# RWKV chunk recurrence: separate 64-row products become stacked 128-row products

## The chip, the cores and the metric

The kernel runs on one core of a Trainium2 chip, in one launch. The metric is the device time in microseconds; lower is better. All data is fp32 in memory.
## The reference

The model has two layers on 256 tokens of width 2048. Layer 0 has eight heads of stick-breaking attention and sixteen heads (of 64 channels) of an RWKV-7 recurrence; layer 1 is a gated delta net; each is followed by a squared-ReLU MLP of width 8192. Only the RWKV part matters here:

```python
def step(S, inp):
    r_t, w_t, k_t, v_t, kk_t, a_t = inp
    s_kk = jnp.einsum('bhij,bhj->bhi', S, kk_t)
    S = (S * w_t[:, :, None, :] - s_kk[..., None] * (kk_t * a_t)[:, :, None, :]
         + v_t[..., None] * k_t[:, :, None, :])
    return S, jnp.einsum('bhij,bhj->bhi', S, r_t)
xs = tuple(jnp.moveaxis(t, 1, 0) for t in (r, decay, k, v, kk, a))
_, y = lax.scan(step, jnp.zeros((bsz, h, n, n), jnp.float32), xs)
```

The kernel computes this in chunks of 64 tokens. With b = kk * a and the decays folded into the operands, a chunk needs the masked grams of (b, kk), (b, r), (k, kk) and (k, r), the inverse of a triangular matrix made of the first (found level by level, from X and A), the corrections U, and then, chunk after chunk, U from the state, the new state from b x U and k x V, and the output y from the state, U and V.

## The kernel before, in words

TensorE's main work is the weight projections. Weights stream from memory in units of two 128-row blocks (`raw`), ScalarE rounds a unit to fp32r (`wh`, L861), VectorE takes the rest (`wl`, L1301), and TensorE makes three products for each pair (L405). In the first layer's group stage a unit is 384 columns wide and a half of a unit is nine products. The splits run two units ahead of TensorE.

RWKV is done for two heads at a time, in eight groups. One group is the generator `mix0(m)`, written once for TensorE, once for ScalarE and once for VectorE. `interleave` and `drive` run each engine's generator between its projection work: `HOPS0` says how many shares of the projection stand behind each `yield`. All order inside an engine is thus fixed in the program. Groups 0 to 6 run beside the projections of the next group, group 7 beside the output projection.

Inside `mix0`, TensorE makes the grams (L512, L518) in 64x64 tiles, one head per 64 rows; VectorE masks them into `GM` (L1477); TensorE transposes b, k, v and kk times decay (L529) and ScalarE copies them to `tok` in two copies (L961, L962). Then come five levels, each with A x X (L544), VectorE's mask of it (L1494), the product with X transposed (L559), VectorE's addition (L1499) and a transpose of X (L536), which ScalarE copies (L967, L975). L565 is A x V. L582 and L588 make the corrections U and W. The four chunk steps are, for chunk c (64 tokens, t = c // 2, hf = c % 2): L599, kk times decay x state, from which VectorE makes U (L1514); L607 and L608, b x U and k x V into one accumulator, from which VectorE makes the new state (L1521, or L1523 and L1526); L611, state x r; L614 and L615, U x gram and V x gram for each head. At the end ScalarE copies y to `yT` (L990), and a chain of means, squares and scales over all three engines ends the group: L621, L622, L1529, L993, L625, L996. The next group's first product (L476) waits for the end of this chain, `rw_o`.

`to_tiles` and the tuples `QUADS` set the order in which the four 64x64 quadrants of the array are used. In the chunk steps the old code has these lines:

```python
mm(mb[3][:, 0:P], tok[R, 0, t, :], U[R, :], start=True, stop=False, skip_group_check=True)
mm(mb[3][:, 0:P], tok[R, 1, t, :], tok[R, 2, t, :], start=False, stop=True,
   skip_group_check=True).then_inc(S("dS"), 1)
```

Of the kernel before, what the change touches and what calls it, by code (L numbers as in the profile page):

```python
# [19 lines left out]
P = 128  # L20
# [140 lines left out]
def trunk(nc, stop, x, w384, w512, wba, consts, c0, c1, prm0, lora, conv, rows1, normw, ln, out):  # L161
    ctx = ExitStack()
    with ctx:
# [78 lines left out]
        XT0 = lay(4 * HC).rearrange("p (h f c) -> p h f c", h=2, f=2)  # L242
        Yn0 = r2(lay(4 * 32), a=4)
        Sa, Sb, U = (lay(P) for _ in range(3))
# [123 lines left out]
        def _(pe):  # L368
            mm = nc.tensor.matmul

            def to_tiles():

                pe.sem_inc(S("tiles"), 1)
# [93 lines left out]
            def mix0(m):  # L467
# [39 lines left out]
                to_tiles()  # L507
                for t in range(TT):
                    for w, src in enumerate((bt, kt_)):
                        for h, hf in QUADS:  # L510
                            at = slice(t * P + HC * hf, t * P + HC * hf + HC)
                            last = mm(mb[h][half(hf), (2 * t + w) * P:(2 * t + w + 1) * P], src[half(h), at],  # L512
                                      KR[half(h), hf, :, t, :], start=t + w == 0, stop=True, skip_group_check=True)
                last.then_inc(S("gram"), 1)
                for t in range(TT):
                    for h, hf in QUADS:
                        at = slice(t * P + HC * hf, t * P + HC * hf + HC)
                        last = mm(mb[2 + h][half(hf), t * HC:(t + 1) * HC], KR[half(h), hf, 0, t, :], bt[half(h), at],  # L518
                                  start=t == 0, stop=True, skip_group_check=True)
# [5 lines left out]
                for w, src in enumerate((bt, kt_, rkv[:, 2, :], None)):  # L525
                    for t in range(TT):
                        e = 2 * w + t
                        src_t = KR[:, t, 0, :, :].rearrange("p t c -> p (t c)") if src is None else src[:, t * P:(t + 1) * P]
                        last = nc.tensor.transpose(mb[e // 4][:, (e % 4) * P:(e % 4 + 1) * P], src_t, ident)  # L529
# [10 lines left out]
                def a_times_x(lv):  # L540
                    for h in range(2):
                        for hf, t in QUADS:
                            Xp = X0[half(hf), 2 * h + t, :].rearrange("p (b w s) -> p b w s", w=2, s=1 << lv)
# [49 lines left out]
                for c in range(4):  # L593
# [8 lines left out]
                    if c == 0:  # L602

                        pe.wait_ge(S("WT_ready"), m1)
# [1383 lines left out]
```

## Time and profile before

| | |
|---|---|
| median of 3 runs | 3163.69 us (3161.73 to 3166.78) |
| the profiled execution, its own time | 3166.6 us |
| its span, first to last instruction | 3164.9 us |
| TensorE busy | 3013.9 us, 95% |
| VectorE busy | 1785.6 us, 56% |
| ScalarE busy | 1420.2 us, 45% |
| mean granted TensorE clock | 0.987 |

A busy figure is a sum over stages with different limits, so it says little about one stage. The eight RWKV groups lie between about 71 and 632 us of the span. A timeline row gives the start in us, the time in us (of the whole row, where several like instructions are merged), the engine, the line, and, for TensorE, the tile shape of the weights and the shape of the moving operand. The distance between the starts of two rows is what an instruction holds the engine for; the time given for one is longer, because instructions overlap in the pipeline. An idle time ahead of a row stands in brackets with what ended it.

### The profile page before, as it was taken

To read this page: it belongs to the slowest core of one execution; us is meant where nothing else is said; L and a number is where in the kernel's file an instruction comes from. 1 tells how busy PE (TensorE), PEld (TensorE's weight loads), DVE (VectorE), ACT (ScalarE), POOL (GpSimd) and SP (SyncE) were. 2 spreads that over 40 slices of the span, in tenths; PEclk is the share of its full clock that TensorE was granted. 3 is DMA by queue.
4 is the path that set the end of the run, shared out by engine and by line. 5 is a ranking of instruction groups with operands and counts; after the bars stand their busy time and mean duration, and the time that the engine had idled before them with its cause. 6 is when DMAs were issued, how large, how long until landed. Compare 5 with 4: busy or idle time off the path is not lost.

```text
span 3164.9 us, 61290 instructions
## 1 busy us (share of the span) xinstructions
PE 3013.9 (95%) x24324; PEld 2731.8 (86%) x24324; DVE 1785.6 (56%) x2390; ACT 1420.2 (45%) x2121; POOL 13.1 (0%) x28
## 2 busy tenths in 40 slices
PE   8899998989999999999999999999998999999997
PEld 8778877789898989889898887899877989898996
DVE  4555565475454555564566666566567545555455
ACT  4444343334343444433555555455554434444442
POOL 0000000000000000000000000000000000000000
PEclk9999999999999999999999999999999999999999
DMA  6333333455555555544333334443335555555553
GB/s 225 98 102 101 98 100 122 143 204 187 192 182 191 185 190 186 187 164 141 114 122 133 121 119 142 160 147 122 113 127 192 181 193 186 193 184 190 187 186 113
DMA packets 157013, 492.35 MB, mean 156 GB/s; under 512 B 15584, under 2 KB 50528, under 8 KB 155776
## 3 DMA queue, kind: packets, MB, share of 16 engines
q1 hardware_dynamic: 154032, 476.18, 44.3%
q0 software_dynamic: 2224, 11.89, 1.0%
q8 instruction: 181, 2.97, 0.4%
q10 hardware_dynamic: 544, 1.05, 0.1%
q14 instruction: 32, 0.26, 0.0%
HBM read 486.96 MB, written 2.10 MB: 155 GB/s over the span
## 4 chain that ended last, share of the span: by engine, by line
PE 79%; DVE 10%; ACT 5%; issue 4%; DVEq 0%; DMA 0%; ACTq 0%; SPq 0%
PE pp L405 70%; DVE wl L1301 2%; DVE ws L1647 2%; ACT wh L861 1%; PE mp L789 1%; PE mp L753 1%; PE mp L737 1%; PE mp L729 1%; PE mp L795 1%; ACT ws L1119 0%; ACT ws L1160 0%; ACT ws L1117 0%; PE mp L447 0%; PE mp L536 0%; DVE xres L1375 0%
## 5 line engine op out<-in xcount | busy, mean ns | idle before, releaser
L1301 DVE TENSOR_TENSOR wl<-raw,wh 128x1024 fp32r<-128x1024 f32 (+1 forms) x936 | 1101.0, 1184 | 942.1 <-ACT wh L861 934.6
L861 ACT CAST wh<-raw 128x1024 fp32r<-128x1024 f32 (+1 forms) x936 | 943.1, 1017 | 928.6 <-PE pp L405 927.7
L405 PE MATMUL pp<-aTh,wh 128*128 128x256 f32 x4400 | 1289.6, 293 | 38.9 <-DVE wl L1301 20.8
L405 PE MATMUL pp<-aTl,wh 128*128 128x256 f32 x4400 | 1250.5, 284 | 0.0
L405 PE MATMUL pp<-aTh,wl 128*128 128x256 f32 x4400 | 1249.9, 284 | 0.0
L405 PEld LDWEIGHTS pp<-aTh,wh 128*128 128x128 f32 x4400 | 849.1, 193 | 59.9 <-issue 24.8
L405 PEld LDWEIGHTS pp<-aTl,wh 128*128 128x128 f32 x4400 | 850.1, 193 | 2.2 <-issue 1.4
L405 PEld LDWEIGHTS pp<-aTh,wl 128*128 128x128 f32 x4400 | 849.0, 193 | 0.0
L405 PE MATMUL pp<-wh,hTh 128*128 128x512 f32 x1408 | 560.1, 398 | 17.2 <-DVE hTl L1677 7.8
L405 PE MATMUL pp<-wh,hTl 128*128 128x512 f32 x1408 | 550.5, 391 | 0.0
L405 PE MATMUL pp<-wl,hTh 128*128 128x512 f32 x1408 | 550.3, 391 | 0.0
L405 PEld LDWEIGHTS pp<-wh,hTh 128*128 128x128 f32 x1408 | 265.7, 189 | 75.7 <-DVE hTl L1677 8.6
L405 PEld LDWEIGHTS pp<-wh,hTl 128*128 128x128 f32 x1408 | 265.4, 189 | 56.4
L405 PEld LDWEIGHTS pp<-wl,hTh 128*128 128x128 f32 x1408 | 265.8, 189 | 52.8 <-issue 0.5
L1194 ACT COPY ws<-mp 128x512 f32<-128x512 f32 x48 | 28.1, 586 | 154.5 <-PE mp L729 154.5
L1647 DVE SCALAR_TENSOR_TENSOR ws<-ws 128x256 f32<-128x256 f32 x192 | 80.0, 477 | 1.0 <-ACT ws L1109 1.0
L1350 DVE TENSOR_TENSOR xres<-xres,pp 128x1024 f32<-128x1024 f32 x36 | 43.7, 1214 | 25.2 <-PE pp L405 25.1
L1596 DVE TENSOR_TENSOR ws<-ws 128x1024 f32<-128x1024 f32 x32 | 39.2, 1225 | 25.3 <-ACT hTh L1062 25.3
L1125 ACT ACTIVATE ws<-mp,ws 128x128 f32<-128x128 f32 x128 | 36.4, 367 | 36.4 <-PE mp L789 36.2
L447 PE MATMUL mp<-cc,xres 128*128 128x128 f32 x128 | 25.5, 352 | 27.2 <-DVE xres L1379 19.5
L1748 DVE TENSOR_TENSOR ws<-mp,cc 128x256 f32<-128x256 f32 x40 | 17.0, 424 | 59.8 <-PE mp L737 59.8
L975 ACT COPY ws<-mp 128x256 f32<-128x256 f32 x40 | 15.0, 375 | 75.9 <-PE mp L536 75.9
(283 smaller groups left out, 1864.4 us busy)
## 6 DMA issues: line engine op xcount, KB each, us to landing
raw<-in_w_dram SPq DMA_DIRECT2D x800, 512.0 KB, 3.6
raw<-in_w_dram SPq DMA_DIRECT2D x136, 384.0 KB, 3.5
ws<-in_ln_dram POOLq DMA_DIRECT2D x8, 1024.0 KB, 7.5
out_dram<-xres SPq DMA_DIRECT2D x8, 256.0 KB, 2.0
ws<-in_lora_dram POOLq DMA_DIRECT2D x8, 192.0 KB, 2.6
xres<-in_x_dram ACTq DMA_DIRECT2D x2, 512.0 KB, 6.1
xres<-in_x_dram SPq DMA_DIRECT2D x2, 512.0 KB, 7.0
ws<-in_c_dram POOLq DMA_DIRECT2D x1, 768.0 KB, 7.5
```

Source lines behind the costliest of these rows:

```text
L405: last = mm(o, lhs, rhs, start=opens and m == 0, stop=end and kk == 1 and m == 2, skip_group_check=True)
L729: last = nc.tensor.transpose(mb[2][:, h * P:(h + 1) * P], Xc[:, 2 * h:2 * h + 2, :].rearrange("p c t -> p (c t)"), ident)
L737: last = mm(mb[hf][half(c), h * P:h * P + 32], At[half(hf), c, h, half(hf)], Xp[:, :, 0, :], start=h == 0, stop=True, skip_group_check=True)
L753: last = mm(mb[2 + c][half(hf), h * P:h * P + 32], XTc[half(c), h, hf, :], Yn1[half(c), 4 * hf + h, :], start=h == 0, stop=True, skip_grou ...
L789: last = mm(bank[:, h * P:(h + 1) * P], lhs[:, h, :], rhs[:, h, :], start=h == 0, stop=True, skip_group_check=True)
L795: last = mm(bank[:, j * T:(j + 1) * T], lhs[:, j, :], rhs[:, 2 * j:2 * j + 2, :], start=j == 0, stop=True, skip_group_check=True)
L861: nc.scalar.copy(wh[:, q % RING, :, 0:width], raw[:, q, :, 0:width]).then_inc(S("hi_ready"), 1)
L1125: last = go(dst[:, h, :], bank[:, h * P:(h + 1) * P], ACT.Copy, scale=scale(h))
L1301: tt(wl[:, q % RING, :, 0:width], raw[:, q, :, 0:width], f(wh[:, q % RING, :, 0:width]), ALU.subtract).then_inc(S("lo_ready"), 1)
L1350: tt(o, o, r2(pp[buf][:, :], a=TT), ALU.add).then_inc(S("evacuated"), 1)
L1596: tt(hid, hid, hid, ALU.mult).then_inc(S("hid_sq"), 1)
L1647: last = stt(qkv[:, j, :], cbuf[:, j, k:T + k], cw[:, bass.ds(g, 1), 4 * j + k], qkv[:, j, :], ALU.mult, ALU.add)
```

## The change

b is stored rotated by one chunk (`btr`, written by VectorE in two parts, 192 and 64 columns), so that b of a chunk lies in the other half of the rows than k of the same chunk after the transposes. U of a chunk then lies below or above V of that chunk in one 128-row operand `UV`, and b and k in `BK`; the two masked grams of a chunk stand on top of each other in `GM` in the same way. With this:

- b x U + k x V is one product of 128 rows (`BK` x `UV`) instead of two of 64.
- U x gram + V x gram of both heads is one product of 128 rows and 128 columns instead of four 64x64 products. It computes the cross terms of the heads too, and they are not read.
- state x r is written for each half of the columns, so two products instead of one (both in full shape, 64 columns each).
- kk x state of chunks 1 and 2 is made with 128 output rows instead of 64; chunk 3 stays at 64.
- The products with b in the quadrants go to the other half of the output rows, which turns the order in which quadrants are used.
- ScalarE's two copies of 512 columns behind the transposes become six: two of 64 partitions (256 columns), one of 256, then a semaphore, then 64 partitions of 512, 384 and 128 columns, then the semaphore again. The transpose of X waits for the first, the second level for the second.
- `yT` is copied in two parts of 64 partitions each.
- The step counters `PER` go from 11 to 15 and from 24 to 25.

```diff
-        tok = lay(4 * T).rearrange("p (w t c) -> p w t c", w=4, t=TT)
+        BK, UV = (r2(lay(4 * P), a=4) for _ in range(2))
+        tokw = r2(lay(2 * P), a=2)
-        GM = GMf[:, 0:1024].rearrange("p (t h w r c) -> p t h w r c", t=TT, h=2, w=2, r=2)
+        GM = GMf[:, 0:1024].rearrange("p (n h r c) -> p n h r c", n=4, h=2, r=2)
...
+                turned = lambda n: slice((n + 3) % 4 * HC, (n + 3) % 4 * HC + HC)
                 for t in range(TT):
-                    for w, src in enumerate((bt, kt_)):
+                    for w in range(2):
                         for h, hf in QUADS:
-                            at = slice(t * P + HC * hf, t * P + HC * hf + HC)
-                            last = mm(mb[h][half(hf), (2 * t + w) * P:(2 * t + w + 1) * P], src[half(h), at],
-                                      KR[half(h), hf, :, t, :], start=t + w == 0, stop=True, skip_group_check=True)
+                            n, e = 2 * t + hf, 1 - hf
+                            src = kt_[half(h), n * HC:(n + 1) * HC] if w else btr[half(h), turned(n)]
+                            last = mm(mb[h][half(hf if w else e), n * P:(n + 1) * P], src, KR[half(h), hf, :, t, :],
+                                      start=t + w == 0, stop=True, skip_group_check=True)
...
+                        if n < 3:
+
+                            last = mm(mb[0][:, 0:P], KR[:, hf, 0, :, :].rearrange("p t c -> p (t c)"), st_in, start=True, stop=True,
+                                      skip_group_check=True)
...
-                    if c < 3:
-                        mm(mb[3][:, 0:P], tok[R, 0, t, :], U[R, :], start=True, stop=False, skip_group_check=True)
-                        mm(mb[3][:, 0:P], tok[R, 1, t, :], tok[R, 2, t, :], start=False, stop=True,
+                    if n < 3:
+                        mm(mb[3][:, 0:P], BK[:, n, :], UV[:, n, :], start=True, stop=True,
                            skip_group_check=True).then_inc(S("dS"), 1)
-                    if c:
-                        mm(mb[2][:, yc_], st_in, KR[:, hf, 1, t, :], start=True, stop=False, skip_group_check=True)
-                    for h in range(2):
-                        hs = slice(64 * h, 64 * h + 64)
-                        mm(mb[2][hs, yc_], U[R, hs], GM[R, t, h, 0, 1, :], start=c == 0, stop=False, skip_group_check=True)
-                        last = mm(mb[2][hs, yc_], tok[R, 2, t, hs], GM[R, t, h, 1, 1, :], start=False, stop=True,
-                                  skip_group_check=True)
-                    last.then_inc(S("y_psum"), 1)
+                    if n:
+                        for h in range(2):
+                            mm(y_[:, half(h)], st_in, KR[:, hf, 1, t, :], start=h == 0, stop=False, skip_group_check=True)
+                    mm(y_, UV[:, n, :], GM[:, n, :, 1, :], start=n == 0, stop=True,
+                       skip_group_check=True).then_inc(S("y_psum"), 1)
...
-                st(nc.scalar.copy(tok[:, 0:2, :, :], mb[0][:, :].rearrange("p (w t c) -> p w t c", w=2, t=TT)))
-                nc.scalar.copy(tok[:, 2:4, :, :], mb[1][:, :].rearrange("p (w t c) -> p w t c", w=2, t=TT)).then_inc(S("tok_ready"), 1)
+                for i in range(2):
+                    st(nc.scalar.copy(UV[half(i), :, :].rearrange("p (t f) c -> p t f c", f=2)[:, :, i, :],
+                                      r2(mb[0][half(i), 0:T], a=TT)))
+                nc.scalar.copy(tokw, r2(mb[0][:, T:2 * T], a=2)).then_inc(S("tok_ready"), 1)
+                st(nc.scalar.copy(BK[half(0), :, :], r2(mb[1][half(0), :], a=4)))
+                st(nc.scalar.copy(BK[half(1), 1:4, :], r2(mb[1][half(1), 0:3 * P], a=3)))
+                nc.scalar.copy(BK[half(1), 0, :], mb[1][half(1), 3 * P:4 * P]).then_inc(S("tok_ready"), 1)
...
-                tt(bt, bt, pinv, ALU.mult).then_inc(S("operands"), 1)
+                st(tt(btr[:, 0:3 * HC], bt[:, HC:T], pinv[:, HC:T], ALU.mult))
+                tt(btr[:, 3 * HC:T], bt[:, 0:HC], pinv[:, 0:HC], ALU.mult).then_inc(S("operands"), 1)
```

## Rows read from the trace of the kernel before

**Rows 1.** The page, chain that ended last, share of the span by engine

```profile
PE 79%; DVE 10%; ACT 5%; issue 4%; DVEq 0%; DMA 0%; ACTq 0%; SPq 0%
```

**Rows 2.** Stretches: from:to, length, busy us (instructions) by engine, clock, DMA share, GB/s

```profile
137.00:203.00 66.00, 60.02 (x662) 52.49 (x662) 35.97 (x73) 27.04 (x54) 0.54 (x1) 1.00 0.32 98
537.00:632.00 95.00, 94.12 (x671) 72.24 (x669) 49.36 (x74) 37.40 (x58) 0.00 (x0) 1.00 0.41 139
```

**Rows 3.** Waits of TensorE, 137 to 203 us: us in total, times, longest

```profile
PE pp L405 <- DVE wl L1301: 2.7, 2, 1.4
...
PE mp L536 <- ACT ws L962: 0.2, 1, 0.2
```

**Rows 4.** Timeline of TensorE, 183 to 193 us: start, us, what [idle before]

```profile
183.15 0.28 PE L405 MATMUL pp<-aTh,wl 128*128 128x256 f32 x1
...
184.60 0.28 PE L405 MATMUL pp<-aTl,wh 128*128 128x256 f32 x1
...
185.43 0.28 PE L405 MATMUL pp<-aTh,wl 128*128 128x256 f32 x1
...
186.23 0.28 PE L405 MATMUL pp<-aTl,wh 128*128 128x256 f32 x1
...
187.06 0.28 PE L405 MATMUL pp<-aTh,wl 128*128 128x256 f32 x1
187.27 0.49 PE L607 MATMUL mp<-ws 64*128 64x128 f32 x2
...
187.91 0.43 PE L611 MATMUL mp<-ws 128*128 128x64 f32 x2
188.27 0.34 PE L614 MATMUL mp<-ws 64*64 64x64 f32 x4
...
188.88 0.28 PE L405 MATMUL pp<-aTl,wh 128*128 128x256 f32 x1
...
190.72 0.49 PE L607 MATMUL mp<-ws 64*128 64x128 f32 x2 [0.37 <-DVE ws L1514]
...
192.33 0.28 PE L405 MATMUL pp<-aTl,wh 128*128 128x256 f32 x1
```

**Rows 5.** Timeline of TensorE in the second layer, around L789

```profile
1554.15 0.28 PE L405 MATMUL pp<-aTh,wl 128*128 128x256 f32 x1
1554.27 1.05 PE L789 MATMUL mp<-ws 128*128 128x128 f32 x8
1555.08 0.36 PE L405 MATMUL pp<-aTh,wh 128*128 128x256 f32 x1
1555.28 0.28 PE L405 MATMUL pp<-aTl,wh 128*128 128x256 f32 x1
```

**Rows 6.** Timeline of VectorE, chunk 0's state

```profile
184.25 0.34 DVE L1521 SCALAR_TENSOR_TENSOR ws<-mp,ws 128x128 f32<-128x128 f32 x1
```

**Rows 7.** Timeline of ScalarE, VectorE and TensorE, 162 to 166 us

```profile
162.50 0.59 ACT L961 COPY ws<-mp 128x512 f32<-128x512 f32 x1 [5.58 <-PE mp L529]
...
163.46 0.84 ACT L861 CAST wh<-raw 128x768 fp32r<-128x768 f32 x1
...
164.34 0.96 DVE L1301 TENSOR_TENSOR wl<-raw,wh 128x768 fp32r<-128x768 f32 x1 [2.23 <-ACT wh L861]
165.21 0.28 DVE L1494 TENSOR_TENSOR ws<-mp,cc 128x128 f32<-128x128 f32 x1
...
165.68 0.43 PE L559 MATMUL mp<-ws 64*64 64x32 f32 x16
```

**Rows 8.** Timeline of ScalarE, 195 to 197 us

```profile
195.69 0.37 ACT L990 COPY ws<-mp 128x256 f32<-128x256 f32 x1 [5.74 <-PE mp L615]
195.96 0.84 ACT L861 CAST wh<-raw 128x768 fp32r<-128x768 f32 x1
```

**Rows 9.** Timeline of VectorE, 151 to 154 us

```profile
151.53 0.43 DVE L1466 TENSOR_TENSOR ws<-ws 128x256 f32<-128x256 f32 x1
151.87 1.82 DVE L1301 TENSOR_TENSOR wl<-raw,wh 128x768 fp32r<-128x768 f32 x2
```

More of the change, by code:

```diff
@@ L516, in mix0 @@
                     for h, hf in QUADS:
-                        at = slice(t * P + HC * hf, t * P + HC * hf + HC)
-                        last = mm(mb[2 + h][half(hf), t * HC:(t + 1) * HC], KR[half(h), hf, 0, t, :], bt[half(h), at],
-                                  start=t == 0, stop=True, skip_group_check=True)
+                        last = mm(mb[2 + h][half(1 - hf), t * HC:(t + 1) * HC], KR[half(h), hf, 0, t, :],
+                                  btr[half(h), turned(2 * t + hf)], start=t == 0, stop=True, skip_group_check=True)
                 last.then_inc(S("gram_a"), 1)
@@ L524, in mix0 @@
                 pe.wait_ge(S("masked"), m1)
[L525 to L529, printed above, removed]
+                for t in range(TT):
+                    at = slice(t * P, (t + 1) * P)
+                    for bank, q, src in ((0, t, rkv[:, 2, at]), (0, 2 + t, KR[:, t, 0, :, :].rearrange("p t c -> p (t c)")),
+                                         (1, 2 * t, kt_[:, at]), (1, 2 * t + 1, btr[:, at])):
+                        last = nc.tensor.transpose(mb[bank][:, q * P:(q + 1) * P], src, ident)
                 last.then_inc(S("tokT"), 1)
@@ L555, in mix0 @@
                     pe.wait_ge(S("XT_ready"), 6 * m + lv)
+                    if lv == 1:
+                        pe.wait_ge(S("tok_ready"), 2 * m1)
                     to_tiles()
                     for h in range(2):
-                        for t, hf in QUADS:
-                            last = mm(mb[t][half(hf), h * T:h * T + 32], XT0[half(t), h, hf, :], Yn0[half(t), 2 * hf + h, :],
+                        for t, e in QUADS:
+                            last = mm(mb[t][half(e), h * T:h * T + 32], XT0[half(t), h, e, :], Yn0[half(t), 2 * e + h, :],
                                       start=h == 0, stop=True, skip_group_check=True)
@@ L564, in mix0 @@
                             for hf, t in QUADS:
-                                last = mm(mb[2 + hf][half(t), h * T:h * T + HC], GM[half(hf), t, h, 1, 0, :],
-                                          tok[half(hf), 2, t, half(h)], start=h == 0, stop=True, skip_group_check=True)
+                                last = mm(mb[2 + hf][half(t), h * T:h * T + HC], GM[half(hf), 2 * t + hf, h, 0, :],
+                                          UV[half(hf), 2 * t + hf, half(h)], start=h == 0, stop=True, skip_group_check=True)
                         last.then_inc(S("AV"), 1)
@@ L581, in mix0 @@
                     for t, hf in QUADS:
-                        last = mm(mb[2 + t][half(hf), h * T:h * T + HC], XT0[half(t), h, hf, :],
+                        last = mm(mb[2 + t][half(1 - hf), h * T:h * T + HC], XT0[half(t), h, 1 - hf, :],
                                   AVs[half(t), (2 * hf + h) * HC:(2 * hf + h + 1) * HC], start=h == 0, stop=True,
@@ L587, in mix0 @@
                     for t, h in QUADS:
-                        last = mm(mb[t][half(h), half(hf)], tok[half(t), 3, hf, half(h)], XT0[half(t), h, hf, :],
+                        last = mm(mb[t][half(h), half(hf)], tokw[half(t), hf, half(h)], XT0[half(t), h, 1 - hf, :],
                                   start=hf == 0, stop=True, skip_group_check=True)
@@ L989, in mix0 @@
                         act.wait_ge(S("y_psum"), 4 * m1)
-                        nc.scalar.copy(yT, mb[2][:, 0:T]).then_inc(S("yT"), 1)
+                        for i in range(2):
+                            last = nc.scalar.copy(r2(yT[half(i), :], a=4),
+                                                  mb[2][half(i), :].rearrange("p (n h c) -> p n h c", n=4, h=2)[:, :, i, :])
+                            if i == 0:
+                                st(last)
+                        last.then_inc(S("yT"), 1)
                     yield
```

48 lines of the change are left out of this document (24 added, 24 removed).

## The prediction, made before the change was run

> **What bounds the kernel now.** I read the page first. The chain that ended last is 79% TensorE and only 15% VectorE and ScalarE [rows 1], so time taken off TensorE counts unless a wait takes its place. The change touches only the RWKV generator `mix0`, so the next view is the stretches. Seven groups run inside the loop stage at about 66 us each; the eighth runs beside the output projection. In a loop group TensorE is busy 60.02 of 66 us, in the eighth 94.12 of 95 [rows 2]. DMA is at 0.32 and VectorE at 36 of 66 us, so neither carries the stage by its total; what matters is where TensorE's missing 6 us lie. The waits of one group say: 2.7 us for VectorE's weight splits, 0.2 us at the first L536 for ScalarE's copies [rows 3], and 0.37 us at L607 for U [rows 4]. (The rest stands at L529, L501, a later L559 and L536, where the change alters nothing.) The timelines of these places then tell, step by step, what is late. All seven loop groups repeat the same pattern, so one is worked out and multiplied.
>
> **TensorE in the chunk steps.** I count from the start of the last projection product (L405) ahead of a block to the start of the second one behind it, because that distance holds both the entry and the exit of a block. Undisturbed L405 products follow each other every 0.12 us (the second behind chunk 0's block starts at 184.60, the ninth at 185.43 [rows 4]).
> In the body of chunk 1 this distance is 188.88 - 187.06 = 1.82 us [rows 4]. In it the entry to the 64-row products (L607) takes 0.21, and L607, L611 and L614 each start a new tile shape. Compare a block in full 128x128 shape of the same data type: eight passes of L789 (four fp32 products of 128 columns, two passes each) take 0.12 to enter, 0.81 to the next L405 and 0.20 to the second, 1.13 in all [rows 5]. That is 0.12 + 7 x 0.112 + 0.03 + 0.20 for 8 passes, so (my formula) 0.35 + 0.112 x (passes - 1). The new body of chunks 1 and 2 has exactly 8 passes, all in full shape: [b;k] x [U;V] 2, the state times r for each half 4, [U;V] times the gram 2. The four in the middle have only 64 columns but full 128x128 weights; no row here shows such passes in sequence, so they are bounded by half a pass of L789, 0.056, and a whole one, 0.112. I take 0.112, the price if the weights pace them; the other end would be worth 0.2 us a block.
> The steps of one loop group, old minus new:
> chunk 0 body, 184.60 - 183.15 = 1.45 [rows 4], against 4 passes, 0.69: 0.76.
> kk x state of chunk 1 (L599, from 128x64 to full shape), 186.23 - 185.43 = 0.80 [rows 4], against 2 passes, 0.46: 0.34.
> chunk 1 body, 1.82 against 1.13: 0.69.
> kk x state of chunk 2: no projection product follows it, L607 waits for U [rows 4]. Only the entry (0.09) and the second pass (0.05) come earlier: 0.14. The wait stays.
> chunk 2 body, from its start 190.72 to 192.33, 1.61 [rows 4], against 1.13 - 0.12 = 1.01: 0.60.
> chunk 3 has no [b;k] part. Before, it was a full-shape entry, 0.12, and the chunk 1 block from L611 on, 188.88 - 187.91 = 0.97 [rows 4] less its change of shape, about 1.0; now 6 passes, 0.91. That 0.1 doesn't reach the end: it lies in the exit (0.37 before, 0.23 now), and y itself is finished some 0.06 later than now counted from the block's start.
> Sum to the start of chunk 3: 2.53 us a group.
> Whether VectorE keeps up: S0 of chunk 1 is written by L1521, which starts at 184.25 behind a weight split and is done at 184.6 [rows 6]. TensorE will ask for it at 183.15 + 0.69 + 0.84 (seven more L405) + 0.12 = 184.80. That is 0.1 us of room at most; the later states have 0.5 us and more.
> One rule of the Trainium skill bears on the size of this: TensorEngine Tiling (Array Packing), Key Properties, says that changing the tiling mode drains the engine, while separate tiles run in parallel. The trace agrees on the first, 0.21 to enter L607 [rows 4] in place of 0.12 for a full-shape block [rows 5]; by the second alone, without the drain, the change would lose, which is rival 4.
>
> **The quadrant products.** Grams, their 64-column followers, A x X, A x V, X x AV and W are as many as before and in the same 64x64 shape; only the order of the quadrants turns, so that at some five seams a quadrant comes up after two others, not after three. Bounds: 0, and one round of 90 ns at each, 0.4 us. I take 0.03: the four passes of L614, on two quadrants only, fit in 0.34 us [rows 4], so a quadrant is free again soon. The eight transposes are the same eight.
>
> **ScalarE's copies behind the transposes.** Two 512-column copies, 0.48 from start to start (162.50 to 163.46 for both) [rows 7], become six: 2 x 256 columns for U/V, 256 for W's operand, then 512, 384 and 128 for [b;k]. A 256-column copy holds the engine 0.27 (195.69 to 195.96) [rows 8]. On the line through both, 384 columns hold it 0.37 and 128 columns 0.16, so the six hold it 0.27 x 3 + 0.48 + 0.37 + 0.16 = 1.82 against 0.96: 0.86 more. That the U/V copies have only 64 partitions changes nothing in this estimate; it counts columns.
> TensorE's next transpose waits only for the first three, which end about 0.16 earlier than the two now: the 0.2 us wait at L536 goes. But behind the last three stands the weight split L861, behind it VectorE's L1301 (164.34), and VectorE executes that before L1494 (165.21), whose result TensorE takes at 165.68 without any reserve [rows 7]. So L1494 moves to 166.07 and ends at 166.36, and L559 starts at about 166.48: 0.80 later than now. That is the whole effect, for all that follows starts from L559. Bounds: 0 (the delay is absorbed) and 0.95. I take 0.80. The other ScalarE work in the way, the XT copy behind L861, is still done before 165.6 and costs nothing.
>
> **Smaller edits.** b x pinv in two parts (192 and 64 columns) instead of one: L1466 holds VectorE 0.34 for 256 columns [rows 9], which leaves 0.07 fixed; 0.07 more, and the two splits that follow it are what TensorE waits for, so it counts. yT in two copies of 64 partitions: 0.26 more on ScalarE ahead of a split, (the price of its second copy [rows 8]), which pushes the split behind it, VectorE's L1301 after that, and with it L1529, the start of the mean and square chain to L625. About 0.1 of the 0.26 is room there now, so 0.15 later counted from y, with the 0.06 of above 0.2. Bounds 0 and 0.35. The masks, U's negation, the subtraction into UV and the step counters cost what they cost now. No DMA and no queue is touched.
>
> **Sum.** Loop group: -2.53 + 0.80 + 0.20 + 0.07 + 0.03 = -1.43 us; times 7, -10.0. The eighth group: TensorE is 99% busy and its splits stand in other hops, so I take the block savings in full, without the wait of chunk 2 (0.76 + 0.34 + 0.69 + 0.34 + 0.69 + 0.08 = 2.9) and no loss: -2.9. Together -12.9 us. The profiled execution took 3166.6 us (span 3164.9), 2.9 above the median of the three, 3163.7; taken off the median this gives 3150.8 us, 0.41% faster. About 0.2% (6.3 us) is what a measurement here can tell from no change.
>
> **Rivals.**
> 1. The copies cost nothing and the tail neither: the group gains 2.5, in all 17.5 + 2.9, 3143.3 us. Against it: L559 has no reserve in rows 7. Chance 0.08.
> 2. TensorE's gain turns into waits in the chunk steps: with one half-unit of projection between two steps, VectorE's chain (L1521, L1523, U) or a weight split comes last. For it: only 0.1 us of room at chunk 1. Against it: VectorE idles half of the stretch. If a third of the loop gain is left, 7 x 0.5 + 2.9, 3157.3 us. Chance 0.18.
> 3. The loop's period is set by something that I don't see in it (the stream of weights), so that only the eighth group gains: 3160.8 us. Against it: DMA 0.32, and the waits lie where VectorE does mixer work. Chance 0.07.
> 4. Slower: the entry and exit cost isn't tied to the tile shape, and full-shape blocks among fp32r projections pay it too. Then only the streaming counts: 0.112 for each pass of L607, L608 and L611 and about 0.28 for the eight quadrant passes of L614 and L615. Chunk 0 goes from 0.45 + 0.28 to 0.45 and gains 0.28, chunks 1 and 2 go from 0.67 + 0.28 to 0.90 and gain 0.06 each, chunk 3 goes from 0.22 + 0.28 to 0.67 and loses 0.16. That is 0.24 a group against 1.10 of losses: 7 x 0.86 - 0.24, or 5.8 more, 3169.5 us. It decides once a group's gain in the blocks is below 1.1 us. Against it stand rows 5. By the Trainium skill, TensorEngine Tiling (Array Packing), Theoretical Speedup, products small in both dimensions gain from packing, and merging them gives that up; here the merged product replaces 64-row products that were issued in sequence, so I hold to the rows. Chance 0.05.
> The forecast itself, 3146 to 3156 us: 0.62.
>
> **Range and chances.** 3144 to 3160 takes in the forecast, most of 2, the edge of 1 and the bounds of the copies (7 x 0.95 in place of 7 x 0.80) and of the tail. Faster by over 0.2% (below 3157.4): 0.62 + 0.08 + half of rival 2, 0.80. Within 0.2%: the rest of 2, rival 3 and a bit of 4, 0.16. Slower: 0.04.
>
> **What would show it.** In the profile after: the distance around chunk 1's body at 1.13; around chunk 0's at 0.69; TensorE idle about 0.9 us at the first L559, for L1494, in each loop group, in place of the wait at L536; L861 behind the six copies 0.86 later; a group period shorter by 1.4 us. It is wrong if full-shape blocks enter with 0.21, if the 64-column passes pace differently from 0.112, or if new waits for VectorE stand at L599 or L607.

## The result, and the profile after

The changed kernel takes 3168.99 us (median of 20 runs, 3166.49 to 3173.69) against 3162.64 us for the kernel before (20 runs, 3160.32 to 3169.72). The ratio is 1.0017, its 95% interval 1.0010 to 1.0023: a loss of 0.17% where a gain of 0.41% was forecast, and outside the range. Its profiled execution took 3170.89 us, with a span of 3169.2 us and a mean granted clock of 0.984 (before: 3166.6, 3164.9 and 0.987).

**The stage.** The same two stretches as in [rows 2], of the changed kernel:

```profile
137.00:203.00 66.00, 58.35 (x642) 51.95 (x640) 36.03 (x75) 29.35 (x61) 0.54 (x1) 1.00 0.32 98
537.00:632.00 95.00, 92.11 (x651) 72.66 (x650) 51.64 (x79) 40.59 (x66) 0.34 (x1) 1.00 0.43 145
```

TensorE is busy 1.7 us less in a loop group (58.35 against 60.02), but that isn't a shorter group. ScalarE has 2.3 us more to do. What TensorE gained went into waits; of the same loop group:

```profile
PE pp L407 <- DVE wl L1317: 2.7, 2, 1.4
PE mp L564 <- DVE ws L1509: 1.7, 2, 1.2
...
PE mp L631 <- ACT ws L1009: 0.4, 1, 0.4
...
PE mp L539 <- ACT ws L970: 0.2, 1, 0.2
```

L564 and L631 are the new ones (L559 and L625 before). L539 still waits for the copies, as L536 did [rows 3]. (L407 is L405 of before, L617 and L622 are the merged grams and states, L605 is kk x state.)

**The chunk steps**, timeline of TensorE, to be laid beside [rows 4]:

```profile
184.52 0.28 PE L407 MATMUL pp<-aTh,wl 128*128 128x256 f32 x1
184.64 0.38 PE L617 MATMUL mp<-ws 128*128 128x128 f32 x2
184.86 0.39 PE L622 MATMUL mp<-ws 128*128 128x128 f32 x2
...
185.20 0.28 PE L407 MATMUL pp<-aTl,wh 128*128 128x256 f32 x1
...
187.33 0.28 PE L407 MATMUL pp<-aTh,wl 128*128 128x256 f32 x1
187.45 0.38 PE L617 MATMUL mp<-ws 128*128 128x128 f32 x2
187.67 0.56 PE L621 MATMUL mp<-ws 128*128 128x64 f32 x4
188.06 0.44 PE L622 MATMUL mp<-ws 128*128 128x128 f32 x2
...
188.46 0.28 PE L407 MATMUL pp<-aTl,wh 128*128 128x256 f32 x1
...
190.19 0.49 PE L617 MATMUL mp<-ws 128*128 128x128 f32 x2 [0.39 <-DVE ws L1529]
```

Counted as the prediction did, chunk 0's body takes 185.20 - 184.52 = 0.68 us, kk x state of chunk 1 in the same way 186.50 - 186.04 = 0.46, chunk 1's body 188.46 - 187.33 = 1.13. The four 64-column passes hold TensorE from 187.67 to 188.06, about 0.1 each: nearly what a pass of 128 columns takes, as the prediction had assumed.

**The copies**, timeline of ScalarE, VectorE and TensorE where [rows 7] were read:

```profile
162.55 0.76 ACT L968 COPY ws<-mp 64x256 f32<-64x256 f32 x2 [5.58 <-PE mp L532]
163.34 0.37 ACT L970 COPY ws<-mp 128x256 f32<-128x256 f32 x1
163.61 0.58 ACT L971 COPY ws<-mp 64x512 f32<-64x512 f32 x1
164.21 0.48 ACT L972 COPY ws<-mp 64x384 f32<-64x384 f32 x1
164.59 0.26 ACT L973 COPY ws<-mp 64x128 f32<-64x128 f32 x1
164.88 0.83 ACT L867 CAST wh<-raw 128x768 fp32r<-128x768 f32 x1
...
165.74 0.96 DVE L1317 TENSOR_TENSOR wl<-raw,wh 128x768 fp32r<-128x768 f32 x1 [3.58 <-ACT wh L867]
166.62 0.28 DVE L1509 TENSOR_TENSOR ws<-mp,cc 128x128 f32<-128x128 f32 x1
...
167.05 0.43 PE L564 MATMUL mp<-ws 64*64 64x32 f32 x16 [1.22 <-DVE ws L1509]
```

ScalarE's six copies stand in the first five rows (the first row merges two). From the first copy to the weight split ScalarE is held 164.88 - 162.55 = 2.33 us, 0.96 before and 1.82 in the prediction. The chain split, L1317, L1509, L564 is the predicted one; only its size is wrong. The same at the end of the group, beside [rows 8]:

```profile
194.75 0.77 ACT L1002 COPY ws<-mp 64x256 f32<-64x256 f32 x2 [4.80 <-PE mp L622]
195.54 0.83 ACT L867 CAST wh<-raw 128x768 fp32r<-128x768 f32 x1
```

The two halves of yT hold it 0.79 us, 0.27 before and 0.53 in the prediction.

**One loop group, after minus before,** by the starts of the same instructions: 1.32 lost at L564, 2.48 gained over the chunk steps, 0.57 lost from there to L631. That is 0.5 to 0.6 us gained in a group (0.6 here), where 1.43 was forecast. The eighth group gains 2.9, as forecast.

**What no term of the prediction held.** In two of the loop groups a stretch of 3.4 us comes at half clock that wasn't there before; five microseconds of each kernel, of the kernel before and of the changed one:

```profile
219.00:224.00 5.00, 4.52 (x47) 4.33 (x51) 2.27 (x3) 2.26 (x4) 0.00 (x0) 1.00 0.75 235
```

```profile
219.00:224.00 5.00, 4.98 (x27) 4.80 (x28) 2.34 (x3) 1.79 (x3) 0.00 (x0) 0.66 0.66 221
```

The clock is the third number from the right, 1.00 and 0.66: for 3.4 us TensorE is granted 0.50, its 1.2 GHz level. A group that has such a stretch is about 1.5 us longer (65.67 to 65.77 us where the groups without one take 64.17 to 64.20). With both, the first layer's recurrence ends only 2.7 us early.

Then the second layer, whose code is untouched. Its first four groups start at -3.0, -0.7, +1.5 and +3.7 us against the kernel before, and its end stands at +4.1: 6.7 us are lost in the first loop groups, 7.1 in all. TensorE's idle times at the top of these groups, before and after:

```profile
1580.40 0.54 PE L405 MATMUL pp<-aTh,wh 128*128 128x256 f32 x1 [2.84 <-ACT ws L1259]
...
1684.15 0.38 PE L405 MATMUL pp<-aTh,wh 128*128 128x256 f32 x1 [2.83 <-ACT ws L1259]
```

```profile
1577.38 0.40 PE L407 MATMUL pp<-aTh,wh 128*128 128x256 f32 x1 [2.83 <-ACT ws L1275]
1580.45 0.58 PE L407 MATMUL pp<-aTh,wh 128*128 128x256 f32 x1 [1.60 <-issue]
...
1683.47 0.57 PE L407 MATMUL pp<-aTh,wh 128*128 128x256 f32 x1 [2.82 <-ACT ws L1275]
1686.54 0.58 PE L407 MATMUL pp<-aTh,wh 128*128 128x256 f32 x1 [1.42 <-issue]
```

The wait of 2.83 us for ScalarE is in both. Behind it the changed kernel starts a few products and then stands still for 1.4 to 1.6 us with nothing that the profile shows in front of it ("issue"); the granted clock, which falls to 0.50 at about the end of the first wait, stays there for 6.8 us. The stretch 1684 to 1688 of before and of after:

```profile
1684.00:1688.00 4.00, 3.85 (x32) 3.85 (x33) 3.46 (x11) 4.00 (x8) 0.00 (x0) 1.00 0.22 79
```

```profile
1684.00:1688.00 4.00, 2.58 (x13) 2.29 (x12) 4.00 (x13) 2.81 (x6) 0.00 (x0) 0.50 0.18 48
```

And one more line of the page differs, the queue that brings instructions (packets, MB), before and after:

```profile
q8 instruction: 181, 2.97, 0.4%
```

```profile
q8 instruction: 184, 3.01, 0.4%
```

Three of the loop groups draw one packet more each. From the end of the wait for ScalarE in one group to its end in the next (1580.40 to 1684.15 us before, 1577.38 to 1683.47 us after) the same queue has, before and after:

```profile
q8 instruction: 10, 0.16, 0.6%
```

```profile
q8 instruction: 11, 0.18, 0.7%
```

### The profile page after: what moved, and what is told of

It is laid out like the page before. It is cut to its first block, busy times and chain, and to the rows that moved or that the text cites. A ratio compares the mean times of both kernels' runs of the same rounds, so it can differ in the third digit from the quotient of the medians.

```text
span 3169.2 us, 60962 instructions
## 1 busy us (share of the span) xinstructions
PE 3002.4 (95%) x24132; PEld 2732.5 (86%) x24132; DVE 1786.9 (56%) x2398; ACT 1435.5 (45%) x2161; POOL 13.1 (0%) x28
## 4 chain that ended last, share of the span: by engine, by line
PE 80%; DVE 10%; ACT 6%; issue 4%; DVEq 0%; DMA 0%; ACTq 0%; SPq 0%
PE pp L407 71%; DVE wl L1317 2%; ACT wh L867 2%; DVE ws L1662 1%; PE mp L795 1%; PE mp L759 1%; PE mp L743 1%; PE mp L735 1%; PE mp L801 1%; ACT ws L1176 0%; PE mp L449 0%; PE mp L564 0%; DVE xres L1391 0%; DVE xres L1395 0%; ACT ws L1135 0%
## 5 line engine op out<-in xcount | busy, mean ns | idle before, releaser
L1317 DVE TENSOR_TENSOR wl<-raw,wh 128x1024 fp32r<-128x1024 f32 (+1 forms) x936 | 1102.0, 1185 | 964.2 <-ACT wh L867 956.9
L407 PE MATMUL pp<-aTh,wh 128*128 128x256 f32 x4400 | 1291.7, 294 | 43.2 <-DVE wl L1317 20.8
L407 PE MATMUL pp<-aTl,wh 128*128 128x256 f32 x4400 | 1252.9, 285 | 0.0
L407 PE MATMUL pp<-aTh,wl 128*128 128x256 f32 x4400 | 1252.5, 285 | 0.0
L407 PEld LDWEIGHTS pp<-aTh,wh 128*128 128x128 f32 x4400 | 851.6, 194 | 62.0 <-issue 28.9
L407 PEld LDWEIGHTS pp<-aTl,wh 128*128 128x128 f32 x4400 | 851.9, 194 | 2.2 <-issue 1.4
L407 PEld LDWEIGHTS pp<-aTh,wl 128*128 128x128 f32 x4400 | 850.8, 193 | 0.0
L407 PE MATMUL pp<-wh,hTh 128*128 128x512 f32 x1408 | 560.3, 398 | 17.2 <-DVE hTl L1692 7.8
L407 PE MATMUL pp<-wh,hTl 128*128 128x512 f32 x1408 | 550.4, 391 | 0.0
L407 PE MATMUL pp<-wl,hTh 128*128 128x512 f32 x1408 | 550.4, 391 | 0.0
L407 PEld LDWEIGHTS pp<-wh,hTh 128*128 128x128 f32 x1408 | 265.5, 189 | 74.9 <-DVE hTl L1692 8.6
L407 PEld LDWEIGHTS pp<-wh,hTl 128*128 128x128 f32 x1408 | 265.6, 189 | 56.3
L407 PEld LDWEIGHTS pp<-wl,hTh 128*128 128x128 f32 x1408 | 266.0, 189 | 53.1 <-issue 0.5
```

The source lines that it names most:

```text
L407: last = mm(o, lhs, rhs, start=opens and m == 0, stop=end and kk == 1 and m == 2, skip_group_check=True)
L1317: tt(wl[:, q % RING, :, 0:width], raw[:, q, :, 0:width], f(wh[:, q % RING, :, 0:width]), ALU.subtract).then_inc(S("lo_ready"), 1)
```

## The experiments

Three questions: do ScalarE's copies cost what the traces suggest, why do they cost so much, and what takes 7 us in a layer that nobody changed? Differences below are against the kernel before, medians beside runs of it on the same chip.

**1. The [b;k] copies on VectorE.**

```diff
-                st(nc.scalar.copy(BK[half(0), :, :], r2(mb[1][half(0), :], a=4)))
-                st(nc.scalar.copy(BK[half(1), 1:4, :], r2(mb[1][half(1), 0:3 * P], a=3)))
-                nc.scalar.copy(BK[half(1), 0, :], mb[1][half(1), 3 * P:4 * P]).then_inc(S("tok_ready"), 1)
+                st(vcopy(BK[half(1), 1:4, :], r2(mb[1][half(1), 0:3 * P], a=3)))
+                st(vcopy(BK[half(1), 0, :], mb[1][half(1), 3 * P:4 * P]))
+                st(vcopy(BK[half(0), :, :], r2(mb[1][half(0), :], a=4)))
```

> The changed kernel, but the three copies of the [b;k] operand are made by VectorE, which idles from about 162.2 to 164.3 us in a loop group; ScalarE keeps three copies. The rest is the change. Theory copies: in the profile of the changed kernel the first L564 waits 1.2 us more than before because six ScalarE copies hold back the weight split. Then that wait goes, each of the seven loop groups gets 1.3 us shorter and the kernel 9 us faster than the changed one, about 3160 us, unless half-clock stretches fall differently (plus or minus 5). Rival: the wait is set by TensorE itself or by VectorE's queue, then the wait at L564 stays above 0.8 us and the time stays near 3168.

Measured: 3158.61 us against 3164.83, ratio 0.9978 (0.9969 to 0.9987). VectorE makes its three copies from 160.13 us on while ScalarE makes the other three, and its weight split follows at 162.05, 0.44 us after it has become idle. The wait of 1.2 us at the first L564 is gone, each loop group is 1.75 us shorter than before (0.5 to 0.6 in the changed kernel), and the first layer's recurrence ends 15.6 us early. So ScalarE's [b;k] copies took 1.2 us of each loop group, as the theory of the copies had it. The second layer again gives back 8.5 us in its first groups, with idle times of 2.52, 1.69 and 2.99 us put to issue.

**2. Half of yT on VectorE as well.**

```diff
-                        for i in range(2):
-                            last = nc.scalar.copy(r2(yT[half(i), :], a=4),
+                        nc.scalar.copy(r2(yT[half(0), :], a=4),
...
+                    if c == 3:
+                        nc.vector.tensor_copy(r2(yT[half(1), :], a=4),
```

> As the run before, and the second half of y is copied by VectorE beside ScalarE's first half, so the two no longer stand one behind the other. Theory copies: the tail of a group, from L627 to L631, loses the 0.4 us wait for ScalarE and L631 comes 0.5 us earlier counted from L627; another 3.5 us over seven groups, about 3156 us, plus or minus 5 for the half-clock stretches. Rival: the tail is set by the projection products between, then only 0.1 us a group moves.

Measured: 3155.09 us, ratio 0.9964 (0.9950 to 0.9978). The wait at L631 is gone and a loop group is 2.15 us shorter than before, 0.4 more than in experiment 1. The second layer loses 6.8 us here.

**3 and 4. More work, elsewhere.** 27 transposes of 128 columns, whose results nobody reads, in the middle of the first layer's MLP of the changed kernel; four of them in the kernel before.

```diff
+                        if mixer and k == 1 and u == 16:
+                            for _ in range(27):
+                                nc.tensor.transpose(mb[0][:, 0:P], ident, ident)
```

> The changed kernel with 27 transposes of the identity (2.9 us of TensorE work that nothing reads) in the middle of the first layer's MLP, so that the second layer starts when it does in the kernel before. Theory phase: the 7 us that the second layer loses are half-clock stretches, and whether a group gets one hangs on when its idle places fall. Then the second layer falls back by up to 7 us and the whole kernel is faster than the changed one though it does more: about 3165 us. Rival code: the loss hangs on something in the change other than time, then the time is the changed kernel's plus 2.9, 3172 us.

> The kernel before with 4 such transposes (0.44 us) at the same place. Theory phase: the time is not simply 0.4 us more; if the half-clock stretches repeat with the time of a group, the second layer can lose several us, up to 3170 us. Rival code: 3163.1 us, the time of the kernel before plus 0.4.

Measured: 3164.00 us (3160.88 to 3169.01) for the changed kernel with 2.9 us more to do, ratio 0.9998 (0.9989 to 1.0007); the changed kernel's own ratio, taken on another chip, is 1.0017, so this is some 0.19% or 6 us below it. No idle time is put to issue in its second layer. The kernel before with four transposes: 3165.85, ratio 1.0003 (0.9994 to 1.0012), no effect. What the second layer loses thus hangs on something that work put some 0.7 ms earlier can change; two causes were left, when the layer's loops begin, and where their instructions stand in the program.

**5. Time without instructions:** three fp32 products of 512 columns in place of the 27 transposes, 2.7 us. With their weight loads these are 12 instructions where the transposes are 54.

```diff
+                                mm(mb[0][:, 0:WIDE], ident, xres[:, 0, 0:WIDE], start=True, stop=True)
```

> The changed kernel with 3 fp32 products of 512 columns (6 passes, some 2.7 us, nothing reads them) at the place where the run with 27 transposes had its 2.9 us: about the same time, but 12 instructions more in TensorE's program instead of 54. In the changed kernel's trace TensorE stands idle for 1.4 to 1.6 us at the top of three groups of the second layer's loop with nothing to wait for, and the queue of instruction fetches has 3 packets more than before. Theory fetch: the change makes TensorE's program shorter, the loop then lies differently in it and its top is fetched late. Then time alone cures nothing: about 3171 us, with the idle places still there. Theory phase: time alone cures it, 3164 us.

Measured: 3174.29 us (3172.43 to 3176.79), ratio 1.0035 (1.0021 to 1.0048). The same delay, and no cure: the second layer's first four groups go from -4.6 to +7.1 us, the worst of all. When its loops begin doesn't decide.

**6 and 7. Instructions without work:** 144 semaphore increments on TensorE in the changed kernel, and 112 in the kernel before (`to_tiles()` is one increment).

```diff
+                            for _ in range(144):
+                                to_tiles()
```

> The changed kernel with 144 semaphore increments that nobody waits for in TensorE's program at the same place. By my count the change took 48 TensorE instructions out of each of three copies of the group in the program; this puts the length back and adds hardly any work. Theory fetch: the idle places at the top of the second layer's groups go, the 3 packets too, and the time falls to about 3161 us, 2 us below the kernel before. Theory phase: 3169 us or a random few us around it.

> The kernel before with 112 such increments, which move the loop to where the changed kernel has it, if a fetch packet of 16.4 KB (2.97 MB in 181 packets) holds 256 instructions of 64 bytes (my reading of the page's queue rows): 112 is 256 less 144. Theory fetch: idle places of 1.4 us and more at the top of three groups of the second layer, and some 6 us slower than the kernel before, 3169 us. Theory phase: 3164 us as before.

Measured: 3182.19 us (ratio 1.0058, 1.0044 to 1.0071) and 3186.78 us (1.0067, 1.0054 to 1.0081). The increments themselves hold TensorE much longer than I had reckoned, 18.05 and 13.08 us:

```profile
811.73 0.76 PE L407 MATMUL pp<-wh,hTh 128*128 128x512 f32 x1 [18.05 <-issue]
```

(the row is of the changed kernel; the other has the same one with 13.08) so the totals miss what was expected, but the second layer answers clearly. With 144 increments the changed kernel's second layer stands at +15.2 us in its first four groups and at +15.6 at its end: it loses nothing. With 112 the kernel before goes from +13.9 to +20.1: it now has the changed kernel's fault, with the same rows:

```profile
1594.25 0.58 PE L405 MATMUL pp<-aTh,wh 128*128 128x256 f32 x1 [2.83 <-ACT ws L1262]
1597.33 0.37 PE L405 MATMUL pp<-aTl,wh 128*128 128x256 f32 x1 [1.22 <-issue]
```

**8. The same increments with the copies on VectorE.**

> The changed kernel with the copies of [b;k] and of the second half of y on VectorE, and the 144 increments. Theory fetch: the gains add, 3155 less some 7: 3148 us. Theory phase: 3155.

Measured: 3169.67 us, ratio 1.0013 (1.0004 to 1.0022), with 18.04 us in the increments. The second layer's first four groups go from +3.5 to +5.2 only, where they lost 6.8 us in experiment 2. The gains of the copies and of the cure add up, but the increments cost more than both bring: my estimate for the same kernel without their price is 3169.67 - 18.04 = 3151.6 us, where 3148 was expected.

**9 and 10. The cure at a lower price:** the 27 transposes again (16 columns of weights each), with the copies on VectorE and in the changed kernel.

```diff
+                                nc.tensor.transpose(mb[0][0:16, 0:P], ident[:, 0:16], ident)
```

> The changed kernel with the [b;k] copies and half of yT on VectorE (3155.1 us alone), and 27 more transposes of 16 columns' weights in the middle of the first layer's MLP, whose results nobody reads. Theory (place of the second layer's loops in the instruction stream costs about 8 us, as 27 transposes of 128 columns showed in the changed kernel): 3155.1 - 7.9 + 27 x (0.06 to 0.11) = 3149 to 3150 us, no idle time put to issue behind the wait for ScalarE at the top of the second layer's groups. Rival (the 5 us gained by padding the changed kernel were an accident of that kernel's clock): 3156.7 to 3158.1 us, the idle times of 1.2 to 2.4 us still there.

> The changed kernel with the same 27 short transposes. Theory: 3169.0 - 7.9 + 27 x (0.06 to 0.11) = 3162.7 to 3164.0 us, that is at most 0.1% from the kernel before, with the loops' loss gone and the ScalarE losses left. Rival as above: 3170.6 to 3171.9 us.

Measured: 3151.20 us (3147.68 to 3156.86), ratio 0.9957 (0.9945 to 0.9969), and 3164.89 us (3162.67 to 3166.99), ratio 0.9998 (0.9989 to 1.0006). Neither has an idle time put to issue in the second layer; the first one's groups there start at -17.9, -17.2, -17.2, -16.4, where experiment 2 went from -15.2 to -8.4. The short transposes are no cheaper than long ones: from the first of the 27 to the next product it is 2.87 us, and 2.86 with the 128 columns of experiment 3. The first is the fastest kernel of this study, 0.43% faster than the kernel before. The gap to experiment 2 (3.9 us by the medians, 0.07% by the ratios) was measured on two chips and isn't resolved by the intervals; that the second layer no longer loses is read from the traces.

**11. The order of the six copies:** W's operand first, then U/V lower and upper half, then [b;k] upper half (384, 128), lower half (512).

```diff
+                st(nc.scalar.copy(tokw, r2(mb[0][:, T:2 * T], a=2)))
                 for i in range(2):
...
                 st(nc.scalar.copy(BK[half(1), 1:4, :], r2(mb[1][half(1), 0:3 * P], a=3)))
+                st(nc.scalar.copy(BK[half(1), 0, :], mb[1][half(1), 3 * P:4 * P]))
+                nc.scalar.copy(BK[half(0), :, :], r2(mb[1][half(0), :], a=4)).then_inc(S("tok_ready"), 1)
```

> The changed kernel with the six ScalarE copies in another order: W's operand (128 partitions), U/V on the lower half, U/V on the upper, the two [b;k] copies of the upper half (384, 128 columns), the 512 columns of the lower half. Theory (a copy that reads and writes other partitions than a 64-partition one before it does not overlap it and costs 0.12 us more; there are three such seams in place of four): ScalarE is held 0.27 + 0.39 + 0.27 + 0.38 + 0.28 + 0.60 = 2.19 us from the first copy to the weight split, in place of 2.33. Rival (every copy of 64 partitions has that 0.12, whatever stands before it; two of the five are merely shortened by something else): 2.33 us as now.

Measured: 3168.61 us in one run. ScalarE's timeline:

```profile
161.91 0.38 ACT L967 COPY ws<-mp 128x256 f32<-128x256 f32 x1 [5.59 <-PE mp L532]
162.18 0.76 ACT L969 COPY ws<-mp 64x256 f32<-64x256 f32 x2
162.85 0.47 ACT L974 COPY ws<-mp 64x384 f32<-64x384 f32 x1
163.22 0.27 ACT L975 COPY ws<-mp 64x128 f32<-64x128 f32 x1
163.51 0.58 ACT L976 COPY ws<-mp 64x512 f32<-64x512 f32 x1
163.99 0.83 ACT L867 CAST wh<-raw 128x768 fp32r<-128x768 f32 x1
```

The hold is 163.99 - 161.91 = 2.08 us, neither the 2.19 of my theory nor the 2.33 of the rival. The 512-column copy of the lower half holds 0.48 here, in front of a split over all partitions; in the changed kernel, in front of a copy of the upper half, it holds 0.60. So the extra isn't between a half and anything else, but between two instructions that start at different partitions (0 and 64).

**12. kk x state narrow again,** one of the change's parts undone.

```diff
-                        if n < 3:
+                        if n < 0:
```

> The changed kernel, but kk x state of chunks 1 and 2 keeps its 64-row output (128x64 tile) as before the change. Theory (each change of tile shape costs TensorE about 0.2 us, the prediction's term of 0.34 + 0.14): each loop group 0.48 us longer up to the mean of y, 3.4 us over the seven and about 0.4 to 0.7 in the eighth. Rival (the gain in the chunk steps came from the merged grams alone, and the wait for U absorbs the rest): 0 to 0.14 us a group.

Measured: 3170.40 us in one run. By the traces a loop group gains only 0.06 us against before, so it is 0.45 to 0.5 us longer than the changed kernel's; 0.48 was expected. The eighth group gains 2.2 in place of 2.9. The half-clock stretches fall elsewhere in this kernel (10.2 us of them in the first layer's recurrence, 20.5 in the changed one), which hides the loss from the total.

**13. One seam:** order of the copies U/V upper, [b;k] upper (384, 128), U/V lower, W's operand, [b;k] lower; yT upper half first.

```diff
+                st(uv(1))
+                st(nc.scalar.copy(BK[half(1), 1:4, :], r2(mb[1][half(1), 0:3 * P], a=3)))
+                st(nc.scalar.copy(BK[half(1), 0, :], mb[1][half(1), 3 * P:4 * P]))
+                st(uv(0))
+                nc.scalar.copy(tokw, r2(mb[0][:, T:2 * T], a=2)).then_inc(S("tok_ready"), 1)
+                nc.scalar.copy(BK[half(0), :, :], r2(mb[1][half(0), :], a=4)).then_inc(S("tok_ready"), 1)
...
-                        for i in range(2):
+                        for i in (1, 0):
```

> The changed kernel with the six ScalarE copies in the order: upper half of U/V, the 384 and the 128 columns of the upper half of [b;k], lower half of U/V, W's operand (128 partitions), the 512 columns of the lower half; and yT's upper half ahead of its lower half. Refined theory (0.12 us extra exactly where a copy starts at another partition, 0 or 64, than the one right before it; the row of idle time ahead of the first copy hides its own): one seam, so from the first copy to the weight split 0.27 + 0.37 + 0.16 + 0.27 + 0.27 + 0.48 + 0.12 = 1.94 us (2.33 in the changed kernel, 2.08 in the order before), and 0.66 us from the first yT copy to the split behind it (0.79). Rival (0.12 at each entry to the upper half and each exit from it, idle or not, and the last copy pays too): 2.06 to 2.18 us, and 0.79. TensorE waits about 0.7 us longer at L539, and L564 comes about 0.4 us earlier if VectorE's chain behind the split still releases it; a loop group is then 0.4 to 0.5 us shorter than the changed kernel's.

Measured: 3166.62 us in one run. ScalarE's timeline:

```profile
162.89 0.37 ACT L967 COPY ws<-mp 64x256 f32<-64x256 f32 x1 [6.35 <-PE mp L532]
163.16 0.47 ACT L970 COPY ws<-mp 64x384 f32<-64x384 f32 x1
163.53 0.27 ACT L971 COPY ws<-mp 64x128 f32<-64x128 f32 x1
163.82 0.37 ACT L967 COPY ws<-mp 64x256 f32<-64x256 f32 x1
164.09 0.37 ACT L973 COPY ws<-mp 128x256 f32<-128x256 f32 x1
164.36 0.58 ACT L974 COPY ws<-mp 64x512 f32<-64x512 f32 x1
164.84 0.84 ACT L867 CAST wh<-raw 128x768 fp32r<-128x768 f32 x1
...
194.71 0.76 ACT L1003 COPY ws<-mp 64x256 f32<-64x256 f32 x2 [4.79 <-PE mp L622]
195.37 0.83 ACT L867 CAST wh<-raw 128x768 fp32r<-128x768 f32 x1
```

164.84 - 162.89 = 1.95 us (1.94 expected, rival 2.06 to 2.18) and 0.66 for yT (0.66 expected, rival 0.79). A loop group is 1.02 us shorter than before, 0.5 better than the changed kernel's, as expected. TensorE's wait at L539 grows less than expected, from 0.2 to 0.6 us, where 0.7 more was the forecast. The refined theory of the copies holds. The kernel as a whole is still behind the one before (3160.42 us in one run on the same chip), since its second layer loses its 7 us as in the changed kernel.

## Why the prediction was wrong

**The chunk steps: right.** 2.48 us a group up to L627, the mean of y, against 2.53 forecast up to the start of chunk 3 (2.39 up to there); 0.68, 0.46 and 1.13 at the single blocks against 0.69, 0.46 and 1.13. Chunk 2's body came out 0.1 longer than forecast (191.30 - 190.19 = 1.11): its first product, L617, holds TensorE 0.32 behind the wait, 0.22 in chunk 1. Experiment 12 shows the term of kk x state by itself. Rival 4 falls: full-shape blocks enter with 0.12. So does rival 2 as it was put: the gain did turn into waits, but at L564 and L631, and none is new at L605 or L617. Rival 3 falls with experiments 1 and 2, in which the period of the loop follows its copies. (That period is 64.7 us before, not the 66 of the window that the prediction read; no term of its sum uses it.) Of rival 1 nothing held, the copies and the tail cost more than forecast. The eighth group's 2.9 was right to 0.1.

**The quadrants and btr: right.** 0 to 0.09 together, forecast 0.10.

**The copies: the step that failed first.** The chain behind them was right; their own term was too small, by the sentence "That the U/V copies have only 64 partitions changes nothing in this estimate; it counts columns". By columns alone ScalarE would be held 1.82 us; it was 2.33. There are four places where a copy, or the split behind the last, starts at another partition than the instruction before it, each 0.12 dearer (a seam): 1.82 + 4 x 0.12 = 2.30. Experiment 11 has two (2.06 by this sum, 2.08 measured), experiment 13 one (1.94, 1.95). At such a place the copy ahead doesn't overlap the next one: it shows 0.37 for 256 columns, and the next follows 0.39 after its start, when it is over, not 0.27. The Trainium skill has this rule for another engine: "VectorE: DVE Perf Modes", section "Two Vector instructions with no wait between them", says that an instruction whose operand starts in another quadrant of partitions than the last one's in the same memory is held until all earlier ones have finished. That page's quadrants are of 32 partitions; the runs here have starts at 0 and 64 alone, and for these ScalarE does the same, by the rows above. The chain behind the copies was forecast correctly, but L564 came 1.32 us later in place of 0.80, beyond the upper bound of 0.95. And the wait at L539 didn't go: with two seams ahead of it, L970 starts 163.34 - 162.55 = 0.79 us behind the first copy, where 0.54 was counted. The copies' miss is 7 x 0.52 = 3.6 us.

**The tail: the same mistake.** 0.79 for yT's two copies in place of 0.53, and 0.57 us at L631 in place of 0.20 (bound 0.35): 7 x 0.37 = 2.6 us. Of the 0.37, 0.26 is the copies'; the other 0.1 is the gain in chunk 3's exit, which stands in the 2.48 up to L627 and, as the prediction said, doesn't reach the end.

**The second layer: no step at all.** "The change touches only the RWKV generator", says the prediction, and puts all the rest of the kernel at nothing without a look at it. 7.1 us were lost there, the largest single term. Shown is: the loss comes and goes with the number of TensorE's instructions ahead of the second layer's loops, in either kernel (experiments 3, 6, 7, 9 and 10), and not with time alone (experiment 5). Of the 15 kernels profiled here, those eight with 184 or 185 packets in the instruction queue lose 6.3 to 11.7 us over the second layer's first four groups against the kernel before, and the other six with 181 or 182 at most 1.7. The count of packets follows the loop: in each of those eight kernels the first three loop groups have 11 packets each, in each of the other seven 10. And the packets' own records (16,384 bytes each) stand beside the idle times. There are three such idle times in each of the eight kernels, and all 24 end 1.20 to 1.55 us after such a packet has landed, although they last 1.14 to 2.99 us; the one that ends at 1580.45 in the changed kernel follows a packet that ran from 1578.23 to 1579.18. That holds in experiment 5 too, where the profile shows one idle time in place of two, 6.05 to 6.46 us long, and puts it to VectorE. So TensorE stands there waiting for its own instructions. Why a loop that is placed otherwise needs one packet more in each group, and just at its top, is not shown.

**The half-clock stretches: no step either.** Two more in the loop, 2 x 1.55 = 3.1 us. They begin some 5 us ahead of the grams, at L503 (L501 before), right behind two idle times of TensorE, for a weight split of VectorE and for ScalarE (1.42 and 0.55 us at 217.13 and 219.02 in the changed kernel). In which of the middle five of the seven loop groups they fall changes from kernel to kernel, with edits that don't touch that place (in experiment 12 none has one). One thing divides the traces: the three kernels with the recurrence of before (before, experiments 4 and 7) have none in these 15 groups, and there the first of the two idle times is 1.33 to 1.36 us long; the twelve with the change have 14 in 60 groups, and theirs is 1.40 to 1.43 us. The 0.07 us between them is the size of the prediction's term for the second part of btr. Whether it brings the stretches on was not tested, and why just two is open.

The sum: 3.6 + 2.6 + 7 x 0.05 + 7.1 + 3.1 = 16.8 of the 17.2 us between the forecast difference (-12.9) and the one between the two profiles (+4.3).

## What to carry to other kernels

Count for each copy where its partitions start, not only its columns: split a PSUM bank's evacuation by halves, and each change of start on ScalarE costs 0.12 us; group copies by start, begin with the odd half after an idle time, or give a half to another engine. A stage of several chains hands a gain on only where the engine in front of the next wait wasn't made later; so after stacking operands the engine that stacks them is the first to be looked at. And when a part that wasn't touched gets slower, look for idle time put to issue at the tops of loops and compare the instruction queue's packets, in all and for each turn of the loop: a few dozen instructions more, ahead of it, were worth some 6 us here.

## What the runs showed of the hardware that I had not expected

- ScalarE: an instruction that starts at another partition than the one right before it costs 0.12 us more (0.39 and 0.60 in place of 0.27 and 0.48 from start to start); after idle time it costs nothing (in experiment 13 the first copy starts at partition 64 behind an instruction at 0, 0.31 us after the start of the last transpose as in the other kernels).
- TensorE: 144 semaphore increments in a row hold it 18.05 us and 112 hold it 13.08, 0.12 to 0.13 us each.
- A transpose with 16 columns of weights costs TensorE as much as one with 128 (27 hold it 2.87 and 2.86 us).
- The place of a loop in the program decides over up to 3.0 us of idle time at its top in each iteration (experiment 1), which ends 1.2 to 1.55 us after a packet of the instruction queue has landed, and more half clock goes with it (6.8 us in each of three groups, 3.4, none and 3.4 before): in the changed kernel a group loses 2.2 to 2.4 us, of which 1.4 to 1.6 are the idle time itself.
